# A hybrid attention and state-space layer on one core: key products ahead of the state-space pair, key copies ahead of the fourth exponential, and other reorderings

## The reference

```python
q_lat = jnp.einsum('bshn,rhn->bshr', q[..., :QK_NOPE], lw['w_uk'])
sc = (jnp.einsum('bqhr,bkr->bhqk', q_lat, ckv)
      + jnp.einsum('bqhe,bke->bhqk', q_rope, k_rope)).astype(jnp.float32) * SOFTMAX_SCALE
p = jax.nn.softmax(sc, axis=-1).astype(ckv.dtype)      # causal mask before it
o_lat = jnp.einsum('bhqk,bkr->bqhr', p, ckv)
o = jnp.einsum('bshr,rhv->bshv', o_lat, lw['w_uv']) * silu(z_attn)

y_diag = jnp.einsum('bcgls,bgjcls,bcsgjp->bclgjp', cb, decay_in, xdt)
y_off = jnp.einsum('bclgn,bcgjpn,bgjcl->bclgjp', cc, states[:, :-1], jnp.exp(a_cum))
h = jnp.exp(da_t)[..., None, None] * h + jnp.einsum('bgjp,bgn->bgjpn', x_t * dt_t[..., None], b_t)
out = x + _rmsnorm(jnp.concatenate([o_attn, y_ssm], -1) @ lw['w_out'], lw['norm_post'])
```

## Time and profile before

| | |
|---|---|
| median of 3 runs | 500.34 us (500.3 to 502.52) |
| the profiled execution | 500.38 us, its span 498.6 us |
| busy: PE, DVE, ACT, POOL | 483.7, 351.4, 283.0, 92.6 us |
| chain that ended last, by engine | PE 73%, DVE 15%, ACT 5%, issue 3%, POOL 2% |

### The profile page before, as it was taken

One profiled execution on the slowest core, in us unless ns is written; L12 is line 12 of the kernel. 1 busy time (PEld: TensorE's weight loads), 2 busy tenths in 40 slices (PEclk: granted clock), 3 DMA queues, 4 the chain that ended last, 5 costly groups with the idle time before them and its releaser, 6 DMA issues.

```text
span 498.6 us, 12380 instructions
## 1 busy us (share of the span) xinstructions
PE 483.7 (97%) x4756; PEld 423.7 (85%) x4756; DVE 351.4 (70%) x795; ACT 283.0 (57%) x580; POOL 92.6 (19%) x122
## 2 busy tenths in 40 slices
PE   8999999999999999999999998999899999999995
PEld 7999999999999999999999874666566689998883
DVE  4653768693857567555433599698999799998763
ACT  6733412234376474654624995677776869764441
POOL 1641000010000010000000142544555701110500
PEclk9999999999999999999999999999999999999998
DMA  8543222469898989979896331733322676799842
GB/s 284 216 170 122 72 74 96 133 196 359 296 321 285 310 286 306 325 263 326 296 309 219 121 93 53 252 124 115 133 89 95 239 254 208 245 316 388 329 130 84
DMA packets 47852, 106.34 MB, mean 213 GB/s; under 512 B 7881, under 2 KB 13794, under 8 KB 47666
## 3 DMA queue, kind: packets, MB, share of 16 engines
q1 hardware_dynamic: 47650, 105.50, 62.6%
q10 hardware_dynamic: 144, 0.05, 0.1%
HBM read 96.27 MB, written 7.75 MB: 209 GB/s over the span
## 4 chain that ended last, share of the span: by engine, by line
PE 73%; DVE 15%; ACT 5%; issue 3%; POOL 2%; SPq 1%; DMA 1%; DVEq 0%; ACTq 0%; POOLq 0%
PE pm L1794 17%; PE pm L1795 16%; PE pm L1796 16%; PE px L1905 3%; PE px L1930 3%; DVE hring L1430 3%; PE px L2092 2%; DVE u L1180 2%; PE px L1795 1%; PE px L1796 1%; PE px L1794 1%; PE pm L2110 1%; DVE w_lo L1087 1%; POOL hring L1741 1%; PE pm L2080 1%
## 5 line engine op out<-in xcount | busy, mean ns | idle before, releaser
L1794 PE MATMUL pm<-xw_hi,w_lo 128*128 128x260 f32 x520 | 150.5, 289 | 0.0
L1795 PE MATMUL pm<-xw_lo,w_hi 128*128 128x260 f32 x520 | 147.0, 283 | 0.0
L1796 PE MATMUL pm<-xw_hi,w_hi 128*128 128x260 f32 x520 | 146.9, 282 | 0.0
L651 ACT ACTIVATE w_hi<-w_raw 128x1024 fp32r<-128x1024 f32 (+1 forms) x70 | 72.5, 1038 | 81.2 <-PE pm L1796 65.4
L1087 DVE TENSOR_TENSOR w_lo<-w_raw,w_hi 128x1024 fp32r<-128x1024 f32 (+1 forms) x70 | 87.8, 1261 | 31.6 <-ACT w_hi L651 31.5
L1794 PEld LDWEIGHTS pm<-xw_hi,w_lo 128*128 128x128 f32 x520 | 98.0, 188 | 1.6
L1795 PEld LDWEIGHTS pm<-xw_lo,w_hi 128*128 128x128 f32 x520 | 97.9, 188 | 0.1
L1796 PEld LDWEIGHTS pm<-xw_hi,w_hi 128*128 128x128 f32 x520 | 97.9, 188 | 0.0
L1794 PE MATMUL pm<-mix_hi,w_lo 128*128 128x264 f32 x128 | 37.2, 291 | 0.8 <-DVE mixlo_a L1485 0.8
L783 ACT ACTIVATE alpha<-nmh 128x1 f32<-128x1 f32 x16 | 4.7, 295 | 56.1 <-DVE nmh L1193 56.1
L1796 PE MATMUL pm<-mix_hi,w_hi 128*128 128x264 f32 x128 | 36.3, 284 | 0.0
(11 more groups left out here) (315 smaller groups left out, 1098.9 us busy)
## 6 DMA issues: line engine op xcount, KB each, us to landing
page<-in_cache SPq DMA_DIRECT2D x128, 288.0 KB, 4.2
w_raw<-in_w_in SPq DMA_DIRECT2D x32, 512.0 KB, 5.1
w_raw<-in_w_out SPq DMA_DIRECT2D x16, 512.0 KB, 3.9
w_raw<-in_w_tok SPq DMA_DIRECT2D x16, 512.0 KB, 5.8
dec<-ac_dram SPq DMA_DIRECT2D x16, 256.0 KB, 3.6
hring<-in_ssm_state SPq DMA_DIRECT2D x8, 512.0 KB, 6.6
o_ssms<-hring SPq DMA_DIRECT2D x8, 512.0 KB, 6.9
w_raw<-in_w_qb SPq DMA_DIRECT2D x6, 384.0 KB, 2.9
```

Source lines behind the costliest of these rows:

```text
L651: act.activation(w_hi[s][:, 0:n], w_raw[s][:, 0:n], ACT.Copy).then_inc(a_whi, 1)
L1794: pe.matmul(out, wl, xh, start=start, stop=False)
L1795: pe.matmul(out, wh, xl, start=False, stop=False)
L1796: return pe.matmul(out, wh, xh, start=False, stop=stop)
```

## The change

Nine places are reordered, and nothing else is done. No instruction is added or taken away, and no semaphore value that is waited for changes. On PE: in the head loop `keys(h + 2)` stands in front of the first `y_pair`; the transpose of the sample's B and C stands in front of `keys(0)`; `query_lat` comes two contraction steps later. On ACT: `copy_k(s + 2)` stands in front of `exps(s + 1, 3)`; behind the loop `gated_square(7)` goes behind the last copies of probabilities, and `mix_high(7)` in front of `ssm_high(0)`. On DVE: `stack_low(2)` to `stack_low(5)` stand together behind the last head of that stage, `stack_low(7)` moves from in front of the loop into its first pass, and `mix_low(7)` stands in front of `group_scale(2)`.

```diff
@@ ACT, the head loop and behind it
-            exps(s + 1, 3)
             if s + 2 < H:
                 copy_k(s + 2)
+            exps(s + 1, 3)
             copy_pt(s, 2)
...
         copy_pt(H - 1, 1)
-        gated_square(7)
         mix_high(H - 2)
         copy_pt(H - 1, 2)
         copy_pt(H - 1, 3)
+        gated_square(7)
+        mix_high(H - 1)
         ssm_high(0)
-        mix_high(H - 1)
         ssm_high(1)
@@ DVE
                 head(n - 5)
-            if n in (6, 7):
-                stack_low(n - 4)
         state(2 * NCH - 1)
         for h in range(3, 5):
             head(h)
-        stack_low(4)
-        stack_low(5)
+        for h in range(2, 6):
+            stack_low(h)
...
         y_pair(0)
-        stack_low(7)
...
                 head(5)
+                stack_low(7)
...
         gated(H - 1)
+        mix_low(H - 1)
         group_scale(2)
-        mix_low(H - 1)
         group_scale(3)
@@ PE
-                    if (i, r, k) == (18, 0, 3):
+                    if (i, r, k) == (18, 0, 5):
                         query_lat()
...
+        pe.wait_ge(a_cvs, 2)
+        pe.wait_ge(v_cb, 2)
+        pe.transpose(px[0:32, 3, 0:P], cvs[:, 1, 8:12, :], cm[:, M_ID, :]).then_inc(p_bct, 1)
         pe.wait_ge(v_xdt, 2 * NCH)
         keys(0)
         state(2 * NCH - 1)
-        pe.wait_ge(a_cvs, 2)
-        pe.wait_ge(v_cb, 2)
-        pe.transpose(px[0:32, 3, 0:P], cvs[:, 1, 8:12, :], cm[:, M_ID, :]).then_inc(p_bct, 1)
         pe.wait_ge(a_bct, 1)
...
+            if h + 2 < H:
+                keys(h + 2)
             if h in PAIRS:
                 y_pair(PAIRS[h][0])
-            if h + 2 < H:
-                keys(h + 2)
             outs(h, 0)
```

## The result

| | before | changed |
|---|---|---|
| median, both timed side by side | 500.32 us (4 runs, 500.05 to 502.52) | 509.95 us (4 runs, 509.48 to 511.34) |
| the profiled execution | 500.38 us, span 498.6 | 510.32 us, span 508.5 |

The ratio is 1.0187, with a 95% interval of 1.0152 to 1.0223. The direction was forecast, the size was not: 509.95 lies above the range that ended at 508.0. Lines of kernel.py are two lower in the changed kernel from about L1530 on.

The account below looks back on a forecast made before the run. It took PE to bound the kernel up to 300 us and after 384, with a hand-over until 343 and then a DVE-POOL loop. 500.38 − 0.7 + 3.0 + 1.9 − 0.25 + 1.7 = 506.0 us, range 503.2 to 508.0.

Parts of the forecast that it names:

- query transposes: PE near 110 us: transposes two contraction steps later, six matmuls fill a 0.72 us wait; −0.7 us, between −0.75 and 0.
- stack copies on DVE: Later stack_low copies delay ACT's stack_high(7) and, through its queue, PE's small w_uv products; +3.0 us, bounds 2.7 to 3.4.
- heads 0 and 1: Keys ahead of y_pair on PE, and stack_low(7) moved, make DVE's work late; +1.9 us, bounds 1.0 to 2.1.
- heads 2 to 5: Key-copy waits go, but the 10.99 us DVE-POOL loop holds neither key product nor copy; 0 us, 1.8 per head without cover.
- behind the loop: From head 5 to the end, gains on PE and POOL against a later mix_low(7); −0.25 us, between −0.9 and +0.5.
- the clock: PE idles 4.5 us before the small w_uv products, so its clock falls and work behind runs slow; +1.7 us, 0 to 2.5.
- B: Rival: not slower, heads are paced by PE's key-copy waits, 2.7 us come back and the clock stays; 501.6 us, chance 0.08.
- C: Rival: the stack copies cost nothing, if ACT's copy of B and C were not behind stack_high(7); 501.3 us, chance 0.04.
- A: Rival: the clock stays up through the gap, so its 1.7 us term drops out; 504.3 us, chance 0.28.

Follow-up runs that it names:

- e2: Kernel before with only the transposes of the sample queries two contraction steps later; 500.97 us, ratio 0.9985.
- e1: Kernel before with only the low parts (stack_low) of heads 2 to 5 together behind the last state-space head; 505.77 us, ratio 1.0095.
- e5: Changed kernel with ACT alone altered: stack_high(7) behind the second key copy instead of ahead of the copy of B and C; 505.71 us, ratio 1.0081.
- e15: Kernel before with keys ahead of y_pair on PE in heads 2, 3, 4 and copy_k ahead of the fourth exponential on ACT; 500.91 us, ratio 0.9993.
- e9: Changed kernel with the old PE order for head 5 alone, y_pair ahead of the keys again; 508.13 us, ratio 1.013.
- e11: Changed kernel with SP alone altered: the first output weight loaded ahead of the sample state; 508.87 us, ratio 1.0147.
- e6: Changed kernel with eight extra, unneeded matmuls of 512 columns in PE's 4.56 us gap before the small w_uv products; 508.03 us, ratio 1.0137.
- e12: Changed kernel with PE making the keys of head 1 before its wait for the copy of B and C; 508.67 us, ratio 1.0133.
- e4: Changed kernel with the low parts (stack_low) of heads 2 and 3 put back between the states, all else as changed; 505.28 us, ratio 1.0081.
- e3: Kernel before with only the keys ahead of y_pair on PE, in all six heads; 505.4 us, ratio 1.0082.

## Why the prediction was wrong

The profiled run took 510.32 us where the sum gave 506.0. The 4.3 us by steps:

| step of the prediction | forecast | measured | how |
|---|---|---|---|
| query transposes | −0.7 | −0.75 (−1.25 to −0.2) | e2, timed |
| stack copies on DVE | +3.0 | +2.87 | rows, e1, e5 |
| heads 0 and 1 | +1.9 | +2.46 | marks |
| heads 2 to 5 | 0 | 0 | period, e15 |
| behind the loop | −0.25 | +1.3 | marks, e9, e11 |
| the clock | +1.7 | +2.98 (1.54 and a second fall in e9, e11) | rows, e6 |

The rows add up to 8.9 of the 9.9; the remaining 1.0 is what the profile of the changed kernel had lost before 303 us, against the gain of e2 (it is 0.31 late there in place of 0.75 early). DVE's row at 31.09 us already starts at 31.57 in it, ahead of anything that was changed, so about half of it is a difference between executions; the rest is open. The kernels of this document start state(6) anywhere from 302.49 to 304.07.

- **The clock** failed by size. The mechanism was right to the place: PE idle, fall to 0.50, the products behind it at double length. But the price came from "slow for at most some 5 us", and the profile has it at 0.50 from 311 to 317, up to 317.5. The upper bound of 2.5 was too low as well. The reduction "because the small products are partly bound by issue" was worth little: they took 1.94 us against 1.11, 1.75 times as long, the keys 1.9 times. For a single fall 1.7 was near what e9 and e11 show, 1.54, but there a second one follows. The Trainium skill, "TensorE: Matmul & The Clock Gate", section "HAM oscillation — how this bites in real kernels", tells of waits that send PE to half clock over and over. Runs e9, e11 and e12 show it: the clock fell a second time, between 336 and 339 us; in e4 and e5 it fell in head 1 alone, at 332 and 334. I had looked for one gap only, while the forecast itself put more waiting into head 1.
- **Behind the loop** is the step that failed in kind. The text says that the first output weight "lands 1.3 later" and gave that no price, though ACT's hi(NIN), and behind it the exponentials of head 7, stood in the same queue. In the kernel before, SP issued the load at 382.09, and 4.54 us later is 386.6; ACT began its split at 386.57 with no wait listed. There was no slack, and every delay of the last state-space products went straight into ACT's queue. Without that wait (e9) this stretch gives −0.2, the forecast value: the gains were counted rightly, the wait was missed.
- **Heads 0 and 1** were undersized by 0.56, and above the bound of 2.1. Counted from y_pair(0), PE's last score block of head 2 came 1.79 late, not 1.3, for hring took 1.78 us instead of 1.58 and the first maximum of head 2 was 2.0 late instead of 1.7.
- **The range.** Its upper end of 508.0 is called "the forecast with a dearer clock", but the clock's own bound of 2.5 gives 506.8. With every term at its upper bound and heads 2 to 5 at 0 the sum is 508.9, still under the measured 510.32. The six matmuls put in front of the query transposes were priced at the whole wait of 0.72 us and took 0.46 of it. The lower end of 503.2 leaves out the lower bound behind the loop, which would make it 502.5, and B and C add up to a chance of 0.12, not 0.11; nothing hangs on these two.
- **Rivals.** A (the clock stays up) is refuted; so is B, by e15 and e3: without the waits for key copies nothing is gained. C is half right: e5 shows that the copies cost next to nothing when ACT's queue lets B and C pass, which in the changed program it does not.

## What to carry to other kernels

A wait in one engine's in-order queue is paid by whatever stands behind it: here a copy for head 7 held up the small products, and a weight that landed just in time held up the exponentials. When a step is moved, list for each transfer that it releases how much slack its landing had, and price every gap that opens on PE twice, once for its length and once for the clock. A wait that only changes its name (key copies to transposed probabilities) was set by a loop elsewhere, and removing it is worth nothing.

## What the runs showed of the hardware

The granted clock did not follow the length of the gap alone. A gap of 2.35 us in head 1 was passed at 1.00 in the changed kernel, and one of 2.36 in e6; gaps of 2.36 in e4, e9, e11 and e12 and of 2.37 in e5 were not (0.53 over the next 3 us in e4). In e12 the clock first fell only after the 2.84 us gap had ended and 32 products had run at full speed. Nor did the gap fix how long the clock stayed low: behind the same 4.56 us it was back at 317.5 in the changed kernel and before 315 in e9 and e11, worth 2.98 and 1.54 us. In one and the same kernel the mean clock was low in five of six executions and not in the sixth, worth 3 to 5 us: the spread of such a kernel is larger (5.1 us in e12 against 1.6 for before in that session), and a clock term belongs in a forecast as a range. A busy time grows with it too, 3.6 us here, with no instruction added.
